# Seven pair sets in an attention block: projections by seven products of quarters, with operands combined by GpSimd

## The reference

```python
hp = jnp.pad(h, ((0, 0), (0, S_pad - S), (0, 0)))
mq, mk, mv, nq, kc, vc, ksl, vsl, kwn, vwn, gz = _split(hp @ w_in, EVEN_SPLITS)
scale = HEAD_DIM ** -0.5
```

```python
s_own = (jnp.einsum('hqd,hkd->hqk', qm, k_own).astype(f32) * scale
         + tb_moba[:, rel_bucket(d_own)])
p = masked_softmax(jnp.concatenate([s_sel.reshape(MOBA_HEADS, Q, n_k), s_own], axis=-1),
                   jnp.concatenate([m_sel, m_own], axis=-1))
```

## Time and profile before

| | us |
|---|---|
| median of 3 runs (lowest, highest) | 1807.99 (1807.89, 1809.47) |
| profiled execution | 1808.2 |
| its span | 1806.4 |
| TensorE busy | 1774.1 (98%) |
| VectorE busy | 644.5 (36%) |
| ScalarE busy | 366.5 (20%) |
| GpSimd busy | 15.1 (1%) |

### The profile page before, as it was taken

One profiled execution on the slowest core, in us unless ns is written; L12 is line 12 of the kernel. 1 busy time (PEld: TensorE's weight loads), 2 busy tenths in 40 slices (PEclk: granted clock), 3 DMA queues, 4 the chain that ended last, 5 costly groups with the idle time before them and its releaser, 6 DMA issues. The chain is left out here.

```text
span 1806.4 us, 23732 instructions
## 1 busy us (share of the span) xinstructions
PE 1774.1 (98%) x9411; PEld 971.0 (54%) x9412; DVE 644.5 (36%) x1379; ACT 366.5 (20%) x720; POOL 15.1 (1%) x17
## 2 busy tenths in 40 slices
PE   8999999999999999999999999999999999999998
PEld 6755533333333333333333335768995469899843
DVE  1764401101101101011011113544655657746555
ACT  2223311111111111111111113333120022222101
POOL 0000000000000000000000000000000000000000
PEclk9999999999999999999999999999999999999999
DMA  9957899999999999999999999632446553125452
GB/s 376 374 246 311 330 406 428 430 432 431 430 433 431 430 431 433 430 431 433 431 430 433 431 430 337 194 126 97 164 161 236 163 186 141 47 94 167 138 178 102
DMA packets 104529, 556.84 MB, mean 308 GB/s; under 512 B 17576, under 2 KB 32653, under 8 KB 78733
## 3 DMA queue, kind: packets, MB, share of 16 engines
q1 hardware_dynamic: 103540, 554.53, 76.6%
q10 hardware_dynamic: 922, 1.36, 0.2%
HBM read 553.78 MB, written 2.10 MB: 308 GB/s over the span
## 5 line engine op out<-in xcount | busy, mean ns | idle before, releaser
L1504 PE MATMUL ps<-ring,xs 128*64 128x512 f32 x2112 | 466.2, 593 | 6.7 <-DMA ring<-in_w_up 3.7
L1504 PEld LDWEIGHTS ps<-ring,xs 128*64 128x64 f32 x2112 | 150.9, 137 | 310.9 <-issue 293.4
L1566 PE MATMUL ps<-ring,actT 128*64 128x512 f32 x1036 | 229.5, 595 | 0.0
L2428 PE MATMUL ps<-ring 128*128 128x512 f32 x448 | 192.8, 592 | 0.0
L1640 DVE TENSOR_SCALAR hT<-ps 128x512 f32<-128x512 f32 x33 | 22.8, 692 | 445.8 <-PE ps L1504 445.8
L1566 PEld LDWEIGHTS ps<-ring,actT 128*64 128x64 f32 x1036 | 71.5, 137 | 155.6 <-issue 129.6
L2428 PEld LDWEIGHTS ps<-ring 128*128 128x128 f32 x448 | 84.9, 190 | 105.7 <-issue 105.7
L1642 DVE TENSOR_SCALAR hT<-ps 128x512 f32<-128x512 f32 x33 | 22.8, 692 | 265.0 <-PE ps L1504 265.0
L2382 PE MATMUL ps<-hT,ring 128*128 128x128 f32 x768 | 93.4, 275 | 0.2 <-ACT hT L1769 0.2
L2382 PEld LDWEIGHTS ps<-hT,ring 128*128 128x128 f32 x768 | 89.5, 192 | 0.5 <-ACT hT L1769 0.3
L2163 PE MATMUL ps<-hT,ring 128*128 128x256 f32 x320 | 73.8, 384 | 2.7 <-ACT hT L1769 1.4
(11 more groups left out here) (504 smaller groups left out, 1907.8 us busy)
## 6 DMA issues: line engine op xcount, KB each, us to landing
ring<-in_w_gate SPq DMA_DIRECT2D x64, 2048.0 KB, 27.1
ring<-in_w_up SPq DMA_DIRECT2D x64, 2048.0 KB, 25.4
ring<-in_w_down SPq DMA_DIRECT2D x62, 2048.0 KB, 27.9
ring<-in_mlp_w SPq DMA_DIRECT2D x16, 2048.0 KB, 8.5
ring<-in_mlp_w SPq DMA_DIRECT2D x32, 1024.0 KB, 5.5
ring<-in_w_mod SPq DMA_DIRECT2D x8, 2048.0 KB, 11.8
ring<-in_odd_w_in SPq DMA_DIRECT2D x6, 2048.0 KB, 10.0
ring<-in_w_mod SPq DMA_DIRECT2D x16, 512.0 KB, 10.9
```

The source lines that it names most:

```text
L1504: mm = pe.matmul(ps[SLOTS * half:SLOTS * (half + 1), bank, :], xs[:, c % 4, c // 4 * SLOTS:(c // 4 + 1) * SLOTS], weights(v, 8 * part + c) ...
L1566: mm = pe.matmul(ps[SLOTS * half:SLOTS * (half + 1), Y, :], actT[:, f % 4, f // 4 * SLOTS:(f // 4 + 1) * SLOTS], moving, start=(f == 0), s ...
L2428: return pe.matmul(product_bank(layer, n), token, weight, start=(c == 0), stop=(c == PAIRS - 1))
```

## The change

Two of the NSA queries (nq2 and nq3 together), and all MoBA queries, keys and values become seven sets of 256 columns, in this order: nq 1, mq 0, mk 0, mv 0, mv 1, mq 1, mk 1. That is 28 matmuls of 128x128 per set, in banks 6 (products 1, 6, 7, 5) and 7 (2, 4, 3). nq0, nq1 and the four small key and value columns stay as they were.

The sums of operands are made by GpSimd: four multiplications of hT by rb, four sums S, and per set four differences T, 36 instructions of 128x512, all between tiles of SBUF. T has three places (`SET_ROWS` 0, 1, 2), so a set's differences wait until the last set in the same place is through TensorE. VectorE's `query` and `key` for these columns go, and ScalarE's `values`; `set_first` and `set_last` come in their stead on VectorE, around the scalings of softmaxes 2 to 8. TensorE's order around them changes: transposition 3 moves behind hidT, weighting 7 directly behind transposition 7, transposition 10 behind an output product, and scores 10 with transposition 9 behind the first output products. ScalarE takes hidT's activations ahead of transposition 3's copy, and w2's copies ahead of exponentials 5. Some transfers wait for a set instead of a column (nq3: set 0; mv1: set 4; mk3: set 6). The tile probC moves to r2b, because the normed tokens take its place. The odd layer's sets get numbers from 7 on and are otherwise the same.

```diff
-    TILES = ("ksl", "nq0", "nv0", "nv1", "kwn", "kc", "vc", "nq1", "nq2", "hid", "nq3", "hidT", "mq0", "mk0", "w2", "mq1", "mv0",
-             "mv1", "mk1", "mq2", "mk2", "mq3", "pc0", "pc1", "mk3")
-    BY_ACT = ("nv0", "nv1", "mv0", "mv1", "hid", "hidT", "w2")
+    TILES = ("ksl", "nq0", "nv0", "nv1", "kwn", "kc", "vc", "nq1", "hid", "hidT", "w2", "pc0", "pc1")
+    BY_ACT = ("nv0", "nv1", "hid", "hidT", "w2")
     FOX = ("fq0", "fk0", "fq1", "fk1")
-    SETS = (("q", 1), ("k", 1), ("v", 0), ("v", 1), ("q", 2), ("k", 2), ("v", 2), ("q", 3), ("k", 3), ("v", 3))
-    SET_ROWS = (0, 1, 2, 0, 1, 0, 1, 0, 1, 0)
+    EVEN_SETS = (("nq", 1), ("mq", 0), ("mk", 0), ("mv", 0), ("mv", 1), ("mq", 1), ("mk", 1))
+    SETS = EVEN_SETS + (("q", 1), ("k", 1), ("v", 0), ("v", 1), ("q", 2), ("k", 2), ("v", 2), ("q", 3), ("k", 3), ("v", 3))
+    SET_ROWS = (0, 1, 0, 2, 0, 2, 0, 3, 4, 5, 3, 4, 3, 4, 3, 4, 3)
+    EVENS = len(EVEN_SETS)
...
+            twice = rb[:].rearrange("p (a n) -> p a n", a=1).to_broadcast([P, 2, SEQ])
+            pool.wait_ge(turns[0].h_ok, C)
+            pool.wait_ge(st_ok, 1)
+            for k in range(4):
+                pool.tensor_tensor(normed_h[0][:, 2 * k:2 * k + 2, :], hT[:, 2 * k:2 * k + 2, :], twice, ALU.mult).then_inc(set_x, 1)
+            A11, A12, A21, A22 = quarter_tiles(normed_h[0])
+            S = set_x_of[0]
+            pool.wait_ge(set_x, 4)
+            pool.tensor_tensor(S[0], A21, A22, ALU.add).then_inc(set_x, 1)
+            pool.tensor_tensor(S[2], A11, A21, ALU.subtract).then_inc(set_x, 1)
+            pool.wait_ge(set_x, 5)
+            pool.tensor_tensor(S[1], S[0], A11, ALU.subtract).then_inc(set_x, 1)
+            pool.wait_ge(set_x, 7)
+            pool.tensor_tensor(S[3], A12, S[1], ALU.subtract).then_inc(set_x, 1)
+            for n in range(EVENS):
+                B11, B12, B21, B22 = set_quarters(n)
+                T = set_rows[SET_ROWS[n]]
+                pool.wait_ge(set_weights_in(n), 16)
+                if n == 0:
+                    pool.wait_ge(proj_ps, 1 + ORDER.index("nv1"))
+                if n == set_number("mv", 0):
+                    pool.wait_ge(proj_ps, 1 + ORDER.index("hid"))
+                    pool.wait_ge(set_ps, 2)
+                elif set_before(n) is not None:
+                    pool.wait_ge(set_ps, 2 * set_before(n) + 2)
+                pool.tensor_tensor(T[0], B12, B11, ALU.subtract).then_inc(set_wp, 1)
+                pool.tensor_tensor(T[2], B22, B12, ALU.subtract).then_inc(set_wp, 1)
+                pool.wait_ge(set_wp, 4 * n + 1)
+                pool.tensor_tensor(T[1], B22, T[0], ALU.subtract).then_inc(set_wp, 1)
+                pool.wait_ge(set_wp, 4 * n + 3)
+                pool.tensor_tensor(T[3], B21, T[1], ALU.subtract).then_inc(set_wp, 1)
...
-            sp.wait_ge(proj_ps, 1 + ORDER.index("nq3"))
+            sp.wait_ge(set_ps, 2 * set_number("nq", 1) + 2)
...
+            def pair_set(n):
+
+                B11, B12, B21, B22 = set_quarters(n)
+                A11, A12, A21, A22 = quarter_tiles(normed_h[n >= EVENS])
+                T, S = set_rows[SET_ROWS[n]], set_x_of[n >= EVENS]
+                operands = {1: (A11, B11), 2: (A12, B21), 3: (S[3], B22), 4: (A22, T[3]), 5: (S[0], T[0]), 6: (S[1], T[1]), 7: (S[2], T[2])}
+
+                def weights_ready(count):
+                    if n < EVENS:
+                        pe.wait_ge(set_wp, 4 * n + count)
+                    else:
+                        pe.wait_ge(set_w, 4 * (n - EVENS) + count)
+
+                def product(k, opens):
+                    token, weight = operands[k]
+                    held, moved = (token, weight) if SETS[n][0] in VALUES else (weight, token)
+                    for c in range(4):
+                        mm = pe.matmul(set_place(n, k), held[:, c, :], moved[:, c, :], start=(opens and c == 0), stop=(c == 3), skip_group_check=True)
+                    return mm
+
+                if n in (0, EVENS):
+                    pe.wait_ge(set_x, 16 if n else 8)
+                    pe.wait_ge(got_v, place("fk1" if n else "nq1")[2])
+                if n in (1, 2):
+                    pe.wait_ge(got_a, place(("hidT", "w2")[n - 1])[1])
+                if n:
+                    pe.wait_ge(set_sum, 8 * (n - 1) + 5)
+                weights_ready(3)
+                product(1, True)
+                product(6, False)
+                product(7, False)
+                product(5, False).then_inc(set_ps, 1)
+                if n:
+                    pe.wait_ge(set_sum, 8 * n)
+                weights_ready(4)
+                product(2, True)
+                product(4, False)
+                product(3, False).then_inc(set_ps, 1)
...
-            even("nq2", w_nq, 256)
+            pair_set(0)
             scores_n(3, 1, kwnT)
             attn.turn(pe, 2)
...
             weigh_n(2, 1, 0)
-            even("nq3", w_nq, 384)
             scores_n(4, 2, kslT)
-            attn.turn(pe, 3)
             bank = even_bank("hidT")
             pe.wait_ge(got_a, place("hid")[1])
             for h in range(2):
                 mm = pe.matmul(ps[:, bank, h * 64:(h + 1) * 64], hidn[:, h * P:(h + 1) * P], cst(m, "twin"), start=True, stop=True)
             mm.then_inc(proj_ps, 1)
-            pe.wait_ge(m.even_in[2], 16)
-            even("mq0", w_mq, 0)
+            attn.turn(pe, 3)
+            pair_set(1)
             weigh_n(3, 1, P)
-            pe.wait_ge(m.even_in[3], 16)
-            even("mk0", w_mk, 0)
             scores_n(5, 2, kwnT)
             attn.turn(pe, 4)
...
-            even("mq1", w_mq, 128)
+            pair_set(2)
             weigh_n(4, 2, 0)
             scores_n(6, 3, kslT)
             attn.turn(pe, 5)
-            pe.wait_ge(mv_in, 16)
-            tokens(even_bank("mv0"), w_mv, 0, 512, proj_ps)
+            pair_set(3)
             weigh_n(5, 2, P)
...
-            even("mk1", w_mk, 128)
-            even("mq2", w_mq, 256)
+            pair_set(5)
             scores_m(8, 0)
             pe.wait_ge(c_taken, 1)
             attn.turn(pe, 7)
-            even("mk2", w_mk, 256)
             weigh_n(7, 3, P)
-            even("mq3", w_mq, 384)
+            pair_set(6)
             scores_m(9, 1)
             attn.turn(pe, 8)
...
-            even("mk3", w_mk, 384)
             weigh_m(8, 0)
-            scores_m(10, 2)
-            attn.turn(pe, 9)
...
-            pe.wait_ge(got_v, place("mk3")[2])
+            pe.wait_ge(got_v, place("pc1")[2])
             outward(turns[1], (0, 1), (4, 5), first=True)
+            scores_m(10, 2)
+            attn.turn(pe, 9)
+            outward(turns[1], (0, 1), (6, 7))
             weigh_m(9, 1)
-            outward(turns[1], (0, 1), (6, 7))
             scores_m(11, 3)
-            attn.turn(pe, 10)
             pe.wait_ge(attn.stored, 5)
             outward(turns[1], (0, 1), (0,))
+            attn.turn(pe, 10)
             weigh_m(10, 2)
...
+            def set_first(n):
+
+                scale = HD ** -0.5 if SETS[n][0] in QUERIES else 1.0
+                p1, u12, u22, u21 = set_parts[n >= EVENS]
+                v.wait_ge(set_ps, 2 * n + 1)
+                if n:
+                    v.wait_ge(set_sum, 8 * n)
+                v.tensor_scalar(p1, set_place(n, 1), scale, None, ALU.mult).then_inc(set_sum, 1)
+                v.wait_ge(set_sum, 8 * n + 1)
+                v.scalar_tensor_tensor(u12, set_place(n, 6), scale, p1, ALU.mult, ALU.add).then_inc(set_sum, 1)
+                v.wait_ge(set_sum, 8 * n + 2)
+                v.scalar_tensor_tensor(u22, set_place(n, 7), scale, u12, ALU.mult, ALU.add).then_inc(set_sum, 1)
+                v.scalar_tensor_tensor(u21, set_place(n, 5), scale, u12, ALU.mult, ALU.add).then_inc(set_sum, 1)
+                v.wait_ge(set_sum, 8 * n + 3)
+                v.scalar_tensor_tensor(set_out(n)[3], set_place(n, 5), scale, u22, ALU.mult, ALU.add).then_inc(set_sum, 1)
+
+            def set_last(n):
+
+                scale = HD ** -0.5 if SETS[n][0] in QUERIES else 1.0
+                p1, _, u22, u21 = set_parts[n >= EVENS]
+                C11, C12, C21, _ = set_out(n)
+                v.wait_ge(set_ps, 2 * n + 2)
+                v.scalar_tensor_tensor(C11, set_place(n, 2), scale, p1, ALU.mult, ALU.add).then_inc(set_sum, 1)
+                v.scalar_tensor_tensor(C21, set_place(n, 4), scale, u22, ALU.mult, ALU.add).then_inc(set_sum, 1)
+                v.wait_ge(set_sum, 8 * n + 4)
+                v.scalar_tensor_tensor(C12, set_place(n, 3), scale, u21, ALU.mult, ALU.add).then_inc(set_sum, 1)
...
+            set_first(0)
             gate(2, 1)
-            query("nq2", nqT[:, 2, :])
+            set_last(0)
             biased(3, 10)
             gate(3, 1)
-            query("nq3", nqT[:, 3, :])
             biased(4, 12)
+            set_first(1)
             gate(4, 2)
-            query("mq0", mqT[:, 0, :])
-            key("mk0", mkT[:, 0, :])
+            set_last(1)
             biased(5, 12)
-            query("mq1", mqT[:, 1, :])
```

(46 more changed lines are left out.)

213 lines of the change are left out of this document (86 added, 127 removed).

## The result

| | before | after |
|---|---|---|
| median, us | 1807.99 (1807.84 to 1809.47) | 1815.3 (1814.05 to 1815.98) |
| profiled execution: time, span, us | 1808.2, 1806.4 | 1815.98, 1814.2 |
| mean granted clock of TensorE | 0.998 | 0.995 |
| even block, us | 141.1 | 147.0 |

The changed kernel is slower by 0.39%: ratio 1.0039, 95% interval 1.0029 to 1.0049. The forecast was 1806.7 us, with a chance of 0.55 for no change beyond 0.2%, and a range of 1803.2 to 1813.5. It was wrong: the kernel became slower, and the time lies outside the range. The profiled execution of the changed kernel is the longest of its six.

What follows compares the result with a forecast made beforehand. TensorE, busy 98% of the span, was taken as the bound. Work -5.4, waits -1.1 and +2.8 gave -3.7 us; port contention +2.4 made it -1.3, so 1806.7 us, range 1803.2 to 1813.5.

Steps and rivals of the forecast that it cites:

- TensorE's work, -5.4: Even block: columns and value projections worth 49.9 us give way to seven sets of 44.5 us, saving 5.4 us.
- the waits of order, +1.7 net: TensorE in the even block: two old waits go, -1.1 us, and four come with the new order, +2.8 us.
- weightings 7 and 10: Even block: TensorE waits 1.0 us before each, for the copy of the transposition that nothing now covers.
- VectorE's part hidden: Even block: some 1.2 us more VectorE work per set, 8 in all, costs nothing, but only just.
- GpSimd in time: Even block: GpSimd's 46 to 53 us of work is ready before TensorE wants it; lateness is not the danger.
- Port contention at scores 1, +1.2: Softmax 0's scalings wait for GpSimd's instructions on the shared ports, delaying scores 1 by 1.2 us, bounds 0 and 3.8.
- the negations: One-input instructions behind the maxima might wait too, up to 1.27 us each; part of the slower rival's upper end.
- Contention at transposition 3, +1.2: Softmax 3's scaling meets GpSimd's weights for two sets: two waits, about 1.9 us, against 0.7 in hand; 0 to 3.
- The middle between ends of 0 and 3.8: At scores 1, 1.2 us was taken between no delay and three whole-instruction waits, as nearest the trace's two overlaps.
- The second rival: GpSimd retakes the ports between any two VectorE instructions, each waiting a whole one: +4.3 us, 1812.3 us; 24%.
- softmax 1: In the slower rival, its scaling uses up 2.8 us in hand and costs some 1.4 us more.
- the forecast's own bounds: The forecast case with stalls between 0.4 and 6.7 us was given 1804.4 to 1811 us, at 54%.

Runs made afterwards that it cites:

- without sums: Changed kernel with GpSimd's 36 sums and the waits on them left out, TensorE multiplying unsummed tiles: 1805.84 us, ratio 0.9983 to the kernel before.
- both holds: Changed kernel with GpSimd's S1 and weights of set 1 held until softmaxes 0 and 1 are scaled, sets 2 and 3 until 3 and 4: 1805.72 us.
- second hold: Changed kernel with only GpSimd's weights of sets 2 and 3 held until softmaxes 3 and 4 are scaled: 1812.95 us, ratio 1.0025.
- first hold: Changed kernel with only GpSimd's S1 and weights of set 1 held until softmaxes 0 and 1 are scaled: 1808.56 us, ratio 0.9998.
- dummies at scores 1: Changed kernel with ten unused products on TensorE ahead of scores 1, filling all but 0.45 us of the stall: 1814.66 us, ratio 1.0032.

## Why the prediction was wrong

- **TensorE's work, -5.4, and the waits of order, +1.7 net:** right. Forecast together -3.7, measured -3.56 in the block without sums and in that with both holds. Sets took 6.34 to 6.45 us; weightings 7 and 10 waited as forecast (0.89 us of idle time each).
- **VectorE's part hidden, GpSimd in time:** right; no set waited for its sums.
- **Port contention at scores 1, +1.2: the step that failed.** It was 4.8. I let each GpSimd instruction hold VectorE back once and the second large scaling follow the first freely. In the trace each of them waits for a GpSimd instruction again: L1708 and the two L1712, 1.05 + 2.1 = 3.1 us more than before. And I counted only instructions with two tensor inputs. The three of the gates, ahead of softmax 0, have one, were in no term, and waited 2.2 us. The sum is 5.3; VectorE came to the gates 0.5 us earlier in the block than before (12.33 us into it against 12.80), behind a transfer that landed earlier, and the rest is the stall. The text named one-input instructions, but only the negations, and only as part of a tail.
- **Contention at transposition 3, +1.2:** the place right, 2.3 measured, and the size wrong by the same step. The forecast had two waits of 1.9 us in all; L1708 and the two L1712 waited 0.5 and 2.1, and the negation (L1691), which has one input, 0.75. Of these 3.3 us 0.8 were in hand.
- **Missing term: TensorE's clock, +2.5.** It was put at nothing without a reason: no sentence weighed what a stall does to the granted clock, though a stall of some us was one end of the range.
- **The middle between ends of 0 and 3.8** was the mistake in method. Both overlaps of the earlier trace rows were of one VectorE instruction; they could not tell whether a second goes through, and half-way was not what they were nearest to. The second rival had the mechanism and 24%; its 1812.3 was low by the gates' instructions and the clock, and high by softmax 1, which cost nothing (with the second hold alone the block is 7.1 us over that with both, of which 4.8 and 2.3 stand at scores 1), and by 0.7 at transposition 3. There is also a slip in the forecast's own bounds: stalls of 0.4 us give 1804.7, not 1804.4.

Sum by measured terms: 141.1 - 3.6 + 4.8 + 2.5 + 2.3 = 147.1 against 146.98. The spans of the two profiled executions differ by 7.8 us, so outside the block 1.9 us are left. The block starts 1.0 later; that start varies from 1118.7 to 1122.5 among these kernels, whose first block has the same code. From the block's end to the span's end every changed kernel takes 545.5 to 545.6 us, that before 544.6 (one profile of each); the attention of the odd block stands where it stood, and the last MLP product of the kernel with both holds ends as far behind the block as before. The microsecond comes after it, where the DMA view has one instruction packet on q14 that the kernel before has not there. What causes it was not tried.

## What to carry to other kernels

Before work goes to GpSimd, list every VectorE TENSOR_TENSOR and TENSOR_SCALAR from SBUF to SBUF, one-input ones included, that runs beside its two-input instructions and ends on TensorE's path; give each up to the length of one GpSimd instruction, and only then subtract what is in hand. (Reciprocals, reductions and evictions from PSUM passed freely here.) Where GpSimd has slack, holding its instructions until the scalings are through was free; making them half as long removed 2.9 of the 4.8 us. A stall of some us on TensorE has a second price in the clock, which may turn up at another stall than the one removed; so read the granted clock of every place after each edit.

## What the runs showed of the hardware

- Beside back-to-back two-input GpSimd instructions of 1.27 us, VectorE got through one SBUF instruction at a time: 0.17 us became 1.22, two that take 1.03 together took 3.12. One-input TENSOR_SCALARs waited too (0.19 to 0.84; two of 0.37 together to 1.92). A reciprocal (0.45), reductions (two in 1.01) and PSUM evictions (four in 1.72) did not. GpSimd's instructions waited for VectorE's as well (1.27 to 1.44 and 1.71).
- Beside one-input GpSimd instructions of 1.49 us the same VectorE instructions took 0.17 and 1.03 us at softmax 0, and at most 0.4 us more elsewhere (the scalings of softmax 1, 1.43).
- The granted clock fell to 0.50 behind idle times of 4.75 and 1.84 us. Behind one of 2.0 us it fell where it had been 1.00 throughout (first hold; dummies at scores 1), and not where it had fallen 30 us earlier (the changed kernel). So the same stall cost 1.3 to 1.5 us in two kernels and nothing in a third; why it did not there was not tried.
